# Two of the eight high parts behind each LayerNorm made on VectorE instead of ScalarE

## What is computed

```
def _layer_norm(z, g, b, out_dtype):
    z32 = z.astype(jnp.float32)
    mu = jnp.mean(z32, axis=-1, keepdims=True)
    var = jnp.mean(jnp.square(z32 - mu), axis=-1, keepdims=True)
    return ((z32 - mu) * lax.rsqrt(var + LN_EPS) * g + b).astype(out_dtype)

def _modulate(x, mods, k):
    return x * (1 + mods[:, 3 * k + 1, None, :]) + mods[:, 3 * k, None, :]
...
    h = _modulate(x, mods, 0)
    y = _swiglu(h, ffn_w_in[i, 0], ffn_w_out[i, 0])
    x = _layer_norm(ALPHA * x + 0.5 * mods[:, 2, None, :] * y, ln_g[i, 0], ln_b[i, 0], dtype)
```

## Time and profile before

| | us |
|---|---|
| median of 3 runs | 2160.38 |
| lowest and highest of them | 2151.51, 2161.56 |
| the profiled execution: time, and span of its trace | 2157.71, 2156.0 |
| TensorE busy (share of the span) | 2112.7 (98%) |
| VectorE busy | 1203.2 (56%) |
| ScalarE busy | 787.7 (37%) |
| GpSimd busy | 246.7 (11%) |

### The profile page before, as it was taken

The page is one execution under the profiler, slowest core; times in us unless marked ns, Lnnn a source line. Parts: engine busy times, 40 slices in busy tenths (PEclk is TensorE's granted clock), DMA queues, the critical chain, the costliest instruction groups (busy, mean ns, idle before and its releaser), DMA issues. The chain is left out here.

```text
span 2156.0 us, 30858 instructions
## 1 busy us (share of the span) xinstructions
PE 2112.7 (98%) x10759; PEld 1734.3 (80%) x10759; DVE 1203.2 (56%) x1878; ACT 787.7 (37%) x1086; POOL 246.7 (11%) x238
## 2 busy tenths in 40 slices
PE   7999999999999999999999999999999999999997
PEld 5788888878878888888888888878778788888886
DVE  6766665556557666655535533577576555333344
ACT  4221222454444222223532222376666545322222
POOL 0000000431122000001300000151111222000002
PEclk9999999999999999999999999999999999999999
DMA  9766752233326657633335532342222123323322
GB/s 314 219 180 204 210 175 73 81 108 96 98 69 186 185 180 228 194 108 108 88 97 179 163 97 72 95 118 77 58 68 68 40 69 96 90 82 113 97 73 83
DMA packets 405669, 266.34 MB, mean 124 GB/s; under 512 B 9416, under 2 KB 366184, under 8 KB 405608
## 3 DMA queue, kind: packets, MB, share of 16 engines
q1 hardware_dynamic: 405608, 265.57, 41.3%
HBM read 263.37 MB, written 2.19 MB: 123 GB/s over the span
## 5 line engine op out<-in xcount | busy, mean ns | idle before, releaser
L832 DVE TENSOR_TENSOR w_lo<-raw,w_hi 128x1024 fp32r<-128x1024 f32 (+2 forms) x384 | 435.0, 1134 | 701.4 <-ACT w_hi L600 700.7
L600 ACT ACTIVATE w_hi<-raw 128x1024 fp32r<-128x1024 f32 (+2 forms) x384 | 371.6, 969 | 1099.6 <-PE ps L1471 1062.5
L1469 PE MATMUL ps<-h_hi,w_hi 128*128 128x512 f32 x1744 | 689.3, 395 | 3.6 <-DVE g L841 2.2
L1471 PE MATMUL ps<-h_hi,w_lo 128*128 128x512 f32 x1744 | 679.4, 390 | 0.0
L1470 PE MATMUL ps<-h_lo,w_hi 128*128 128x512 f32 x1744 | 678.9, 389 | 0.0
L1469 PEld LDWEIGHTS ps<-h_hi,w_hi 128*128 128x128 f32 x1744 | 327.3, 188 | 80.3 <-issue 9.8
L1471 PEld LDWEIGHTS ps<-h_hi,w_lo 128*128 128x128 f32 x1744 | 327.3, 188 | 69.3
L1470 PEld LDWEIGHTS ps<-h_lo,w_hi 128*128 128x128 f32 x1744 | 327.6, 188 | 67.1 <-issue 1.4
L1469 PE MATMUL ps<-g_hi,w_hi 128*128 128x512 f32 x704 | 276.0, 392 | 0.0
L1471 PE MATMUL ps<-g_hi,w_lo 128*128 128x512 f32 x704 | 274.1, 389 | 0.0
L1470 PE MATMUL ps<-g_lo,w_hi 128*128 128x512 f32 x704 | 274.0, 389 | 0.0
(11 more groups left out here) (251 smaller groups left out, 1969.5 us busy)
## 6 DMA issues: line engine op xcount, KB each, us to landing
raw<-in_ffn_w_in_dram SPq DMA_DIRECT2D x176, 512.0 KB, 3.7
ada_raw<-in_ada_w_dram SPq DMA_DIRECT2D x128, 512.0 KB, 4.3
raw<-in_ffn_w_out_dram SPq DMA_DIRECT2D x64, 384.0 KB, 3.4
raw<-in_ffn_w_out_dram SPq DMA_DIRECT2D x64, 320.0 KB, 3.1
raw<-in_hgrn_w_in_dram SPq DMA_DIRECT2D x40, 512.0 KB, 3.6
raw<-in_na_w_qkv_dram SPq DMA_DIRECT2D x24, 512.0 KB, 3.7
boot<-in_ada_w_dram SPq DMA_DIRECT2D x8, 512.0 KB, 7.4
boot<-in_ada_w_dram SPq DMA_DIRECT2D x16, 256.0 KB, 6.0
```

Of the source, the lines that this page charges most:

```text
L600: nc.scalar.activation(w_hi[s][:, 0:ph.kt, :], raw[s][:, 0:ph.kt, :], ACT.Copy).then_inc(S.w_hi_done, 1)
L832: nc.vector.tensor_tensor(w_lo[s][:, 0:ph.kt, :], raw[s][:, 0:ph.kt, :], w_hi[s][:, 0:ph.kt, :].bitcast(F32), ALU.subtract).then_inc(S.w_l ...
L1469: nc.tensor.matmul(ps[:, bank, :], w_hi[s][:, k, :], a, start=start and k == 0, stop=False)
L1471: ins = nc.tensor.matmul(ps[:, bank, :], w_lo[s][:, k, :], a, start=False, stop=stop and k == ph.kt - 1)
```

## The change

VectorE makes `h_hi` of tiles 0 and 1 itself, with a `tensor_scalar` (x times A plus B, both read as one value per partition) right behind `normalise` of the tile. ScalarE leaves these two out: it begins with `whole(0)` and `whole(1)`, then waits until VectorE's two high parts have been counted, and goes on as before with tiles 2 to 7. `low_parts` and `next_residual` now also wait for the high part of their tile, since another engine may have made it. The same is done at all five seams.

```
+DVE_HIGH = 2
...
-                high(0)
-                whole(0)
-                high(1)
-                whole(1)
+                for k in range(DVE_HIGH):
+                    act.wait_ge(S.norm_done, n * KT + k + 1)
+                    whole(k)
+                act.wait_ge(S.h_hi_done, n * KT + DVE_HIGH)
                 high(2)
                 for k in range(3, KT):
                     high(k)
...
             def low_parts(n, k):
                 dve.wait_ge(S.h32_done, n * KT + k + 1)
+                dve.wait_ge(S.h_hi_done, n * KT + k + 1)
...
+                def high(k):
+                    dve.wait_ge(S.norm_done, (n + 1) * KT + k + 1)
+                    nc.vector.tensor_scalar(h_hi[:, k, :], x[:, k, :], A[:, n + 1, k:k + 1], B[:, n + 1, k:k + 1],
+                                            ALU.mult, ALU.add).then_inc(S.h_hi_done, 1)
+
...
                 normalise(0)
+                high(0)
                 dve.wait_ge(S.mean_copied, n + 1)
                 for k in range(1, DVE_CENTRED):
                     centre(k)
                     normalise(k)
+                    if k < DVE_HIGH:
+                        high(k)
...
                 for k in range(KT):
                     pool.wait_ge(S.h32_done, (n + 1) * KT + k + 1)
+                    pool.wait_ge(S.h_hi_done, (n + 1) * KT + k + 1)
```

## The result

| | before | after |
|---|---|---|
| median, lowest, highest (us) | 2158.55, 2151.51, 2161.56 (10 runs) | 2169.80, 2163.88, 2171.77 (10 runs) |
| profiled execution: time, span | 2157.71, 2156.0 | 2168.87, 2167.2 |

The ratio of after to before is 1.0053, with a 95% interval from 1.0043 to 1.0063: 11.3 us, half a percent slower. The profiled executions differ by 11.2 us, so the two traces hold the whole loss. The time lay inside the predicted range, 2.7 us above the forecast of 2167.1, but this flatters it: the forecast started from a median of before that came out 1.8 us lower with more runs, and the loss is 11.3 us where the sum said 6.7. One execution of the kernel before that took 7509.57 us, among the 15 beside experiment 9, was in the slow state and is left out of the ratio there.

A forecast was written before the change was run, and what follows sets the result against it. TensorE was taken to bound the kernel, with VectorE setting the pace at the seams. Seam losses of 1.6 + 0.9 + 0.9 + 1.8 + 1.5 = 6.7 us on a median of 2160.4 gave 2167.1 us; range 2157 to 2175.

The forecast's parts named there:

- What bounds the kernel: Whole kernel: TensorE busy 2112.7 of 2156.0 us, so the change pays or costs only by moving its matmuls at five seams.
- GpSimd in the way: At the seams, VectorE's tensor_scalar on SBUF waits for GpSimd's running centring, coming out 0.29 to 0.39 us behind it.
- The price of a high part without it: VectorE's queue at a seam: each added tensor_scalar costs at least 0.54 us, two 1.1 us, without GpSimd's hold-up.
- Rival A: GpSimd doesn't stand in the way: low part 0 1.1 us later, seams +2.8 us, 2163.2 us; chance 0.22.
- high part 0: VectorE at a seam: ready 0.71 us after normalise(0) starts, GpSimd's first centring ends at 0.80, out at 1.19.
- rival B: High part 0 loses the first gap too, out at 2.4; 1.4 us more a seam, +13.8, 2174 us; chance 0.10.
- the place of the centrings: GpSimd at a seam: centres tiles 4 to 7 from -0.47 to 4.59 us around normalise(0)'s start, 1.26 us each.
- High part 1: VectorE at a seam: ready at 2.52, held by GpSimd's third centring until 3.45, out at 3.84 us.
- What follows from the delay: Low part 0 1.81 us later; TensorE loses 1.6, 0.9, 0.9, 1.8 and 1.5 us at the five seams.
- The waits for high part 1: TensorE at the first seam: h_hi 1 usable at 3.99 us, against 3.91 when TensorE came to it before.
- Rival C: New stalls lower TensorE's clock once more at the seams: 0.9 us more each, +11.2, 2171.6 us; chance 0.07.

The follow-up runs named there:

- experiment 9: Kernel before, VectorE's slot-3 weight conversion moved behind low part 0, five unread matmuls in TensorE's idle gap at the two mixer seams; 2153.64 us, 0.9984.
- experiment 4: Kernel before, ScalarE making all eight high parts, with four unread VectorE instructions a seam, two behind normalise(0) and two behind normalise(1); 2166.00 us, 1.0036.
- experiment 1: Changed kernel, with GpSimd starting its four centrings only when VectorE's two high parts are done; 2169.52 us, 1.0058.
- experiment 3: Changed kernel, high parts made by a scalar_tensor_tensor with its second tensor in PSUM, leaving out B; 2160.30 us, 1.0019.
- experiment 5: Changed kernel with VectorE making only h_hi 0, h_hi 1 being ScalarE's again; 2161.98 us, 1.0019.
- experiment 6: Changed kernel with a small unread GpSimd memset ahead of its four centrings, to start them a little later; 2169.27 us, 1.0057.

## Why the prediction was half right

**What bounds the kernel: right.** The loss is where TensorE's matmuls at the five seams came later, and nowhere else. ScalarE's two activations less gained nothing (experiment 4 has them all and follows the same line).

**GpSimd in the way: right.** That its centrings hold up VectorE's `tensor_scalar` was argued from one line; experiments 1 and 3 show it. The price of a high part without it was right, too: 0.54 us of the queue at least, said the text, and in experiment 1 the step from one `normalise` to the next `centre` went from 0.61 to 1.18, so 0.57. Rival A, GpSimd as a bystander, had low part 0 1.1 us later and a sum of +2.8; by the line through the experiments that delay would be 5.5 - 2.0 = 3.5.

**The failed step: high part 0.** "`high(0)` is ready at 0.71; GpSimd's first centring ends at 0.80; out at 1.19." It was ready at 0.73, and out at 2.27 to 2.29 in the second, fourth and fifth seams and at 2.04 in the other two. In the three seams the step took the gap between two centrings for the moment at which the one ends in the trace. What the runs show is that the gap closes earlier: a centring starts every 1.26 us, a `tensor_scalar` asked for 1.12 us behind the start of one still got through (experiment 5), and from 1.18 us on the next centring had it. "0.09 us ahead of the gap" was 0.1 us too late. In these three seams this was rival B, with a chance of 0.10; its argument against ("`tensor_scalar` went first in rows 10") rested on a row in which the instruction had waited through the whole of GpSimd's, and so said nothing on one that comes at the last moment.

In the first and third seam another term of the same step failed, the place of the centrings. It had them from -0.47 on, which held for all five seams of the kernel before; in the changed kernel, where the clock was at 1.00, they began at 0.45. High part 0 came 0.27 us into the first centring and took 1.31. No rival had this case. The two come to nearly the same delay, 2.7 and 2.9 us, and that the forecast was short by about a microsecond at each of the five seams alike is chance.

**High part 1: right in size.** Forecast: ready at 2.52, out at 3.84, 1.32 us in all. Measured: 1.31 to 1.32 in all five seams, only later (3.62 to 4.94 in the second seam), since tile 0 was late. The way there was off by a tenth twice over: it was asked for 0.24 us behind the start of a centring instead of 0.3, and came out 0.29 us behind its end, as in rows 10, instead of the 0.39 that the text allowed for two values per partition.

**What follows from the delay: right.** The forecast's delay of low part 0 was 1.81 us; it was 2.69 to 2.90, on average 1.0 more. Put 1.0 on each of the five terms, 1.6, 0.9, 0.9, 1.8, 1.5, and they become 2.6, 1.9, 1.9, 2.8, 2.5, 11.7 in all, against a measured 2.45, 2.11, 1.90, 2.89, 2.72, 12.07. Not a term of TensorE's side was far off. Rival B had 1.4 more per seam instead of 1.0, so 13.8.

**The waits for high part 1: missed.** The forecast had `h_hi` 1 at 3.99 and no stop there. TensorE waited 1.0 us for it at every seam. It adds nothing of its own, since TensorE stopped again at k = 2 at every seam, for 0.56 to 0.58 us, until ScalarE had `h_hi` 2, and at the first and fourth once more at k = 4 (0.15 and 1.27 us).

**Rival C, a second fall of the clock: did not happen.** The windows of the changed kernel at the first and the fifth seam, with TensorE busy for less than half of a window and the clock at 1.00:

```profile
416.00:418.00 2.00, 0.98 (x5) 0.84 (x5) 1.97 (x3) 0.47 (x1) 2.00 (x2) 1.00 0.27 80
...
1788.00:1790.00 2.00, 0.99 (x5) 0.51 (x4) 1.96 (x3) 0.81 (x1) 2.00 (x3) 1.00 0.00 0
```

**The chances.** The verdict lies at the bound that the text set at half a percent, 10.8 us. Outcomes over it had 0.19, and B, the mechanism that came in three of the five seams, 0.10. A step that turns on 0.09 us between two engines, whose distance varied from 0.46 to 0.55 us in the five seams of the kernel before alone, and by a whole microsecond from one trace to the next, should have been given even odds. That the time came out within the range is owed to the range's width: the sum had 60% of the loss.

## What to carry to other kernels

Before work goes to an engine with much idle time, look at its queue in the stretch concerned, not at its share of the span: VectorE at 56% was the pace-maker of the seams, and a delay of its queue of 14.0 us came back as 12.1. A `tensor_scalar` on SBUF like this one beside a busy GpSimd cost what was left of GpSimd's instruction and at times the whole next one; an instruction of the same size with its second input in PSUM didn't. And the distance between two engines at a seam, read in one trace, is no constant: it went with the clock that TensorE had in the statistics. The thin matmuls of a seam took 1.7 to 1.84 us per eight at the lower level and 0.95 to 1.17 at the full clock; whether filling an idle microsecond ahead of them keeps it up is open.

## What was new about the hardware

**The turn-taking of VectorE and GpSimd.** GpSimd's `tensor_tensor` of 128x512 on SBUF starts every 1.26 us. A high part asked for while one is running ended 1.56 to 1.59 us behind its start (all 23 that were held, in the change and experiments 5 and 6), whether it had been asked for at 0.28 (first seam of the change: 412.72, 413.00 and 1.31 us long) or at 0.94 (fourth seam of experiment 6). The free one takes 0.55, so it would begin at about 1.02. That is an estimate: the `tensor_scalar` of rows 10 ended at 1.57 as well (1522.80 to 1524.37), though it takes 0.43 when free. Asked for at 1.12 it still went first, at 1.18 and later it waited for the next. "SBUF — State Buffer", section "Who interferes with whom", of the Trainium skill says that whoever issues first has the shared pair for the whole instruction while the other is fully blocked. The blocking agrees. By this estimate the hold ends 0.24 us before the next centring starts, and it is taken again between 0.12 and 0.05 us ahead of that one's shown start (two high parts asked for 0.12 to 0.13 ahead went first, one at 0.05 ahead didn't); it was on these tenths that the case turned.

**Two tensors in SBUF on both sides.** In experiment 1 VectorE's low part took 1.18 us beside the centrings and 0.68 without them, and four centrings 6.46 us instead of 5.05. The same section of the Trainium skill says that a VectorE instruction with two SBUF inputs contends with a GpSimd one that reads SBUF; the trace agrees. It isn't a steady slowing of both, the ends hang on each other. The last centring ended at 665.53, 1.15 us behind the end of the first low part (664.38), and the second low part ended at 666.08, 0.55 behind that. The 1.15 and the 0.55 came out the same, to 0.03, at all five seams of this kernel, as if each had to wait for the other to be done or nearly done.

**The clock and the spread of the runs.** The same statistics of a seam took 4.93 us at the full clock (5.14 once), 5.7 to 6.5 when it fell in the course of them, and 8.4 to 8.96 when it fell ahead of them; one seam of experiment 1, with 7.24, lies between. Which of them a seam gets changed from trace to trace with no edit near it. The runs of the kernel before lay between 2151.4 and 2161.6 us, with a mean granted clock of 0.996 in those of 2151.4 to 2151.7 and of 0.991 to 0.992 in those of 2161.1. Ahead of the fifth seam of the kernel before it fell about a microsecond behind the first real matmul after the idle 1.09 us (1764.63). With that gap filled it fell some 4 us behind the same matmul (1762.24 in experiment 9), but with the gap unfilled it also fell 5.2 us behind it (experiment 3) and not at all (experiment 6).
